# A float32 two-block model on one core: in the second attention, where VectorE splits the weights and where one unit is rounded

## The reference

```python
dq, dk, dv, fq, fk, fv = jnp.split(u @ w_in, ATTN_SPLITS, axis=-1)
# 12 dilated heads in 3 groups (window, dilation): softmax with a linear bias by distance
s = jnp.einsum('brnqhd,brnkhd->brnhqk', qc, kb) * (Dh ** -0.5) + bias
lse = logsumexp(s); p = exp(s - lse); o = einsum('brnhqk,brnkhd->brnqhd', p, vb)
alpha = softmax(stack(lses), axis=0)            # weighs the three groups
# 4 differential heads: two softmaxes, the second taken away with weight lam
a = probs(qb1, k1) - lam * probs(qb2, k2);  out = einsum('bhqk,bkhd->bqhd', a, vf)
diff = rms_norm(diff) * (1 - lam_init)
mixed = concatenate([dil_out, diff], axis=2);  return mixed @ w_out
```

## Time and profile before

| | us |
|---|---|
| median of the three runs | 1872.81 |
| the profiled execution, its time | 1872.04 |
| the profiled execution, its span (first to last instruction) | 1870.2 |
| PE busy in the span | 1824.6 (98%) |
| DVE busy | 1477.8 (79%) |
| ACT busy | 1232.8 (66%) |

### The profile page before, as it was taken

One profiled execution on the slowest core, in us unless ns is written; L12 is line 12 of the kernel. 1 busy time (PEld: TensorE's weight loads), 2 busy tenths in 40 slices (PEclk: granted clock), 3 DMA queues, 4 the chain that ended last, 5 costly groups with the idle time before them and its releaser, 6 DMA issues.

```text
span 1870.2 us, 25929 instructions
## 1 busy us (share of the span) xinstructions
PE 1824.6 (98%) x9976; PEld 1558.8 (83%) x9976; DVE 1477.8 (79%) x1502; ACT 1232.8 (66%) x1292; POOL 25.5 (1%) x27
## 2 busy tenths in 40 slices
PE   9989999999899999999999999999999999999998
PEld 7867899887789998987788888888888888888886
DVE  7975688657667765675988988889889899898886
ACT  6966556455654434663777777777777777777775
POOL 0000000000000000000000000000000000000000
PEclk9999999999999999999999999999999999999999
DMA  9422445543235554534699999999999999999994
GB/s 356 158 86 90 158 180 181 202 174 117 73 115 189 187 184 144 185 125 146 229 381 358 391 373 358 375 364 391 376 343 378 374 391 367 341 391 372 379 378 162
DMA packets 69091, 491.97 MB, mean 263 GB/s; under 512 B 7792, under 2 KB 8176, under 8 KB 10096
## 3 DMA queue, kind: packets, MB, share of 16 engines
q1 hardware_dynamic: 67248, 484.33, 68.0%
q0 software_dynamic: 1728, 6.03, 1.6%
HBM read 485.09 MB, written 5.24 MB: 262 GB/s over the span
## 4 chain that ended last, share of the span: by engine, by line
PE 86%; DVE 7%; ACT 5%; issue 2%; POOL 0%; DVEq 0%; ACTq 0%; POOLq 0%
PE ps L424 26%; PE ps L433 20%; PE ps L426 20%; PE ps L435 5%; PE ps L428 5%; DVE wl L2207 2%; PE ps L1370 1%; ACT wh L1450 1%; PE ps L444 1%; PE ps L1271 1%; PE ps L584 1%; DVE hTl L2265 1%; ACT hTh L1488 1%; PE ps L854 1%; PE ps L855 1%
## 5 line engine op out<-in xcount | busy, mean ns | idle before, releaser
L3163 DVE TENSOR_TENSOR wl<-raw,wh 128x2048 fp32r<-128x2048 f32 x334 | 761.2, 2291 | 88.1 <-ACT wh L2089 87.4
L2089 ACT ACTIVATE wh<-raw 128x2048 fp32r<-128x2048 f32 x333 | 637.9, 1918 | 182.5 <-PE ps L433 182.5
L424 PE MATMUL ps<-wh,hTh 128*128 128x512 f32 (+2 forms) x1128 | 443.0, 394 | 5.5 <-DVE hTl L2538 1.5
L426 PE MATMUL ps<-wh,hTl 128*128 128x512 f32 (+2 forms) x1128 | 434.7, 386 | 0.0
L2207 DVE TENSOR_TENSOR wl<-raw,wh 128x2048 fp32r<-128x2048 f32 x124 | 283.6, 2290 | 123.8 <-ACT wh L1450 123.4
L1450 ACT ACTIVATE wh<-raw 128x2048 fp32r<-128x2048 f32 x125 | 238.6, 1914 | 138.0 <-PE ps L433 70.2
L433 PE MATMUL ps<-wl,hTh 128*128 128x512 f32 (+2 forms) x1128 | 300.9, 386 | 0.0
L424 PE MATMUL ps<-wh,work_r 128*128 128x512 f32 x648 | 254.8, 393 | 0.0
L424 PEld LDWEIGHTS ps<-wh,hTh 128*128 128x128 f32 x1128 | 212.0, 188 | 48.8 <-issue 4.2
L426 PE MATMUL ps<-wh,work_r 128*128 128x512 f32 x648 | 252.5, 390 | 0.0
L426 PEld LDWEIGHTS ps<-wh,hTl 128*128 128x128 f32 x1128 | 212.2, 188 | 40.1
(11 more groups left out here) (442 smaller groups left out, 1548.9 us busy)
## 6 DMA issues: line engine op xcount, KB each, us to landing
raw<-in_units SPq DMA_DIRECT2D x458, 1024.0 KB, 6.8
x<-in_x SPq DMA_DIRECT2D x2, 512.0 KB, 5.9
work<-in_lru_w SPq DMA_DIRECT2D x1, 1024.0 KB, 16.0
xn<-in_mem SPq DMA_DIRECT2D x1, 1024.0 KB, 14.2
out<-x POOLq DMA_DIRECT2D x2, 512.0 KB, 6.4
consts<-in_consts POOLq DMA_DIRECT2D x1, 768.0 KB, 4.5
consts<-in_consts SPq DMA_DIRECT2D x1, 356.0 KB, 12.5
cols<-in_cols SPq DMA_DIRECT2D x1, 202.0 KB, 2.6
```

Of the source, the lines that this page charges most:

```text
L424: nc.tensor.matmul(out, sh, mh, start=(first and j == 0), stop=False)
L426: nc.tensor.matmul(out, sl, mh, start=False, stop=False)
L2089: A(wh[:, n % SPLIT, :], raw[:, n % RAW, :], ACT.Copy).then_inc(sem("hi_made"), 1)
L3163: V.tensor_tensor(wl[:, n % SPLIT, :], raw[:, n % RAW, :], wh[:, n % SPLIT, :].bitcast(F32), ALU.subtract).then_inc(sem("lo_made"), 1)
```

## The change

Nine calls change their place, none is added or taken away. On DVE `lo_to(at + 8)` moves behind `biased(3)`, `lo_to(at + 9)` behind `out_copied(0)` and `biased(5)`, `lo_to(at + 10)` behind `out_copied(1)` and `biased(7)`, `lo_to(at + 11)` behind `out_copied(2)` and `biased(9)`, `lo_to(at + 12)` behind `out_copied(3)`, `lo_to(at + 13)` behind `diff_scaled` and `out_copied(D0 + 1)`. Unit 14 (the third of the output projection) is rounded on ACT behind `turned(D0 + 10)` in place of behind `turned(D0 + 6)`, and split on DVE behind `attn_oT_low(1)` in place of ahead of `out_copied(D0 + 6)`.

```diff
@@ ACT
         attn_turned(3, 1)
         turned(D0 + 6)
-        hi_to(at + 15)
         turned(D0 + 7)
         exponentials(16)
...
         turned(D0 + 10)
+        hi_to(at + 15)
         attn_oT_high(1)
         turned(D0 + 11)
         hi_to(at + 16)
@@ DVE
         combined(0)
+        biased(3)
         lo_to(at + 8)
-        biased(3)
         head_scale(1)
         biased(4)
         combined(1)
-        lo_to(at + 9)
         out_copied(0)
         biased(5)
+        lo_to(at + 9)
         biased(6)
         combined(2)
-        lo_to(at + 10)
         out_copied(1)
         biased(7)
+        lo_to(at + 10)
         biased(8)
         head_squares(2)
         combined(3)
-        lo_to(at + 11)
         out_copied(2)
         biased(9)
+        lo_to(at + 11)
         head_scale(2)
         biased(10)
+        out_copied(3)
         lo_to(at + 12)
-        out_copied(3)
         biased(11)
         diff_normed()
         out_copied(D0)
-        lo_to(at + 13)
         diff_scaled()
         out_copied(D0 + 1)
+        lo_to(at + 13)
         out_copied(D0 + 2)
...
         out_copied(D0 + 5)
-        lo_to(at + 15)
         out_copied(D0 + 6)
...
         attn_oT_low(1)
+        lo_to(at + 15)
         out_copied(D0 + 11)
         dilated_mixed(af, 2)
         lo_to(at + 16)
```

## The result

The changed kernel takes **1858.92 us** (median of 4 runs, 1858.38 to 1859.99) against 1872.07 (4 runs) of the kernel before beside it: ratio 0.9929, 95% interval 0.9917 to 0.9941. Measured again in a later set of runs it took 1860.9 (5 runs) against 1871.68 (9 runs), ratio 0.9942 [0.9929, 0.9956]. The forecast was 1861.8, range 1859.5 to 1869.0.

The account below looks back on a forecast made before the run. PE's own work was taken as the bound, with idle waits and half clock recoverable: 7.4 idle + 5.1 clock - 0.9 new wait - 0.6 handovers = 11.0 off 1872.04, plus 0.8 for the median: 1861.8 us, range 1859.5 to 1869.0.

Parts of the forecast that it names:

- the sum: Attention stage: idle time gone 7.4, clock 5.1, new wait -0.9, handovers -0.6, added as separate terms to 11.0 us saved.
- idle time gone: 7.4: Six PE waits ahead of weigh and turn vanish: 1.71 + 0.32 + 2.15 + 2.20 + 0.30 + 0.70 us.
- the 0.6 us that it set aside for handovers: Deducted for handovers with half a microsecond of slack or less, as the one ahead of weigh(0).
- place 2: PE's 2.15 us wait at weigh(D0) for out_copied(3), behind unit 11's rest: gone, with 3 us of slack.
- place 3: PE's 2.20 us wait at weigh(D0 + 2) for out_copied(D0 + 1), behind unit 12's rest: gone, 1.9 us slack.
- new wait at weigh(D0 + 4): PE would wait about 0.9 us there for an unshortened chain on the other engines; bounds 0 and 1.5.
- place 4: PE's 0.30 and 0.70 us waits at 512.79 and 514.83, held by unit 14's rounding and rest: both gone.
- the three middle moves: Rests near scores 5, 7 and 9: PE idles only 0.32 us there, but each gives DVE 2.2 us back.
- I expect full clock in the stage: With no PE idle time over 0.3 us between weigh(0) and weigh(D0 + 2), 5.1 us of clock returns; bounds 0 and 5.1.
- My first rival: Half rate comes anyway, elsewhere in the stage, so only idle time less 0.6 is saved: 1866.0 us; chance 0.21.
- ACT takes DVE's place: ACT's roundings, left in place, end most waits; only the weigh(0) wait goes: 1869.4 us, no change; chance 0.10.
- Unit 14 at the end: Rival: ACT's 0.1 us fit ahead of attn_oT_high(1) fails, costing 7.5 us; slower, 1876.9 us; chance 0.05.

Follow-up runs that it names:

- The filled kernel: Kernel before, with matmuls that nobody reads filling PE's waits ahead of weigh(0), weigh(D0) and weigh(D0+2): 1870.13 us, ratio 0.9987.
- the middle moves alone: Kernel before, with only the rests of units 8, 9 and 10 moved: 1869.47 us, ratio 0.9986.
- the changed kernel without them: Changed kernel with the rests of units 8 to 10 put back where they were: 1863.09 us, ratio to before 0.9956.
- the four kernels with a part of the moves: Kernel before with only unit 14 moved (1869.51 us), only unit 7's rest (1869.40), only rests 11 and 12 (1867.24), only rests 8 to 10 (1869.47).
- the kernel with only the rests moved: Changed kernel with unit 14 put back, so only DVE's rests of units 7 to 12 are moved: 1861.79 us, ratio to before 0.9939.
- the one with the rests too late: Changed kernel with the rests of units 7 and 8 moved too far, together behind combined(2): 1862.21 us, ratio to before 0.9954.

## Why the prediction was off, point by point

The step that failed is the sum. Its term "idle time gone: 7.4" measured 8.5, and the 0.6 us that it set aside for handovers was not due: 12.5 us came back in the stage for 11.0. Of the 2.9 us between 1861.8 and 1858.92, 1.05 is the difference of the profiled runs (12.05 for 11.0). The other 1.8 is a term that no row bears: the median was put 0.8 us above the profiled run, as in the kernel before, and in the changed kernel it lay 1.1 below it. In the later set it lay 2.4 above it (1860.90 and 1858.49), so this part is chance.

By differences of start times between the same instructions in the two profiles (us):

| step | forecast | measured |
|---|---|---|
| wait at weigh(0) gone | 1.71 | 1.88 |
| half rate behind it gone | 1.7 | 1.61 |
| weigh(3) | 0.32 | 0.48 |
| weigh(D0), place 2 | 2.15 | 2.35 |
| weigh(D0 + 2), place 3 | 2.20 | 2.39 |
| half rate behind it gone | 3.4 | 3.13 |
| new wait at weigh(D0 + 4) | -0.9 | -0.88 |
| weigh(D0 + 7), turn(D0 + 8), place 4 | 1.00 | 1.35 |
| unit 14's new place | 0 | 0 |
| set aside for thin handovers | -0.6 | 0 |
| sum (measured: with 0.15 between the steps) | 11.0 | 12.46 |

- **The places** were right: each of the four, the new wait with its size, the fit of unit 14, and ACT's wait ahead of `exponentials(3)` at 2.37 for 2.4.
- **"Idle time gone: 7.4" was mis-sized.** It gave back 8.5, about 0.2 more for each of six waits. The bracket in a row counts from the modelled end of the matmul before, which in a row without a wait overlaps the next start. Of the kernel before: L859 x4 starts at 436.09 and `weigh(0)` at 438.87, 2.78 later; of the changed kernel 436.22 and 437.13, 0.91 later. The wait cost 1.87, not 1.71; and `weigh` itself takes 0.85 behind a wait and 0.78 without one.
- **"0.6 for the handovers" was not due.** The thinnest, at `turned(0)`, held.
- **The range** was too narrow at the bottom by the same terms. Its lower end is added up wrongly: 7.4 + 5.1 + 1 is 13.5, not 13.3, which would be 1859.3, still above the measured median. It was taken off the first median of three, 1872.81; the measured difference was 13.2, but from 1872.07. In the later set it was 10.8, so the miss of 0.6 us is less than what separates two measurements of the same pair.
- **The sum's form was wrong, though its total was near.** It added the clock to the idle time as if each came back alone, and counted the three middle moves as worth 0.3 us, though the prediction itself says of them that each gets back 2.2 us on DVE's side and that several add up. The filled kernel got back 2.3 us of time for 6.7 of clock; the middle moves alone gave 3.0, and the changed kernel without them lost 2.2. In the kernel before the half rate cost little, since PE at full clock would have waited at a later `weigh`: nothing of the first stretch, about 2.2 of the second. It is the moved rests that make full clock worth its share: in the complete change the cover is gone, and there the two terms do add up (1.61 and 3.13 measured). So the total came near partly by luck: the form held only for all moves together. The stages of the four kernels with a part of the moves add up to nearly the whole as well (0.9 + 4.0 + 4.6 + 3.1 = 12.6 for 12.5), and that is no proof of separate terms: the 2.35 us at `weigh(D0)` went both with unit 11's rest and with the middle ones, new waits stand against it, and each profile had its half rate in other places.
- **"I expect full clock in the stage" held in both profiles of the changed kernel, for a reason that is not shown.** "Because nothing of that length is left" is not it: in the kernel with only the rests moved, half rate came behind waits of 0.30 and 0.70 us, and in the one with the rests too late none followed a wait of 2.19. The rule that I set beside the term, from the Trainium skill, TensorE: Matmul & The Clock Gate, Part 1 (the switch falls differently from run to run), is the one that the runs bear out. Behind the same wait of 1.7 us at `weigh(0)`, 1.7 us of clock were lost in the kernel before and with the middle rests moved, 3.4 with unit 14 or the rests of units 11 and 12 moved; behind the 2.15 us at `weigh(D0)` the clock stayed at 1.00 in the kernel before and fell to 0.83 with unit 14 or unit 7's rest moved. My first rival rested on it. What it describes is seen in the kernel with only the rests moved, and in no profile of the changed kernel.

The other rivals: "ACT takes DVE's place" is refuted by the kernel with only the rests moved, since no rounding moved and 10.6 us came back. "Unit 14 at the end" came within 0.16 us of its condition on ACT and did not occur.

## What to carry to other kernels

A long instruction without an urgent reader belongs behind the short steps that others wait for, and in a chain that goes round between three engines it pays even where the profile shows no wait right behind it: what it frees is the pace of that chain. Look for how late it may come by its first reader, since past that point the wait is only moved. And before idle time and lost clock are added up, ask what PE would wait for next if it ran faster.

## What the runs showed of the hardware

- The mean clock of a run moved with the kernel: 0.9922 over 25 runs before, 0.9958 over 10 with the waits filled, 0.995 to 0.997 over 9 of the changed kernel. The two profiles of the changed kernel had no window of the stage under 1.00; outside of it the windows 100 to 110 and 200 to 210 us read between 0.66 and 0.84 in every profile.
- In the later set the changed kernel's time follows its clock (1858.45 and 1858.49 us at 0.996, 1860.90 to 1862.16 at 0.995) and the kernel before's does not (1870.66 to 1872.17 over 0.991 to 0.994, in no order). That there is less waiting left for the half rate to hide in would explain it; it is not shown, and in the first set the changed kernel's four runs are in no such order (1859.99 at 0.997, 1858.38 at 0.996).
- The first half-rate stretch of the kernel before, 1.7 us of missing clock, was hidden whole by the waits behind it: with it gone `weigh(D0)` started 43.18 us behind `turn(0)`, as with it.
- A wait of PE costs about 0.2 us more than the idle time that its row shows: 1.88 for 1.71, 2.35 for 2.15, 2.39 for 2.20.
